# Layer-0 output products of a two-layer decoder trunk: three rounded products each, with split weights streamed through six slots

## The reference

```
h = x
for layer in range(2):
    hn = rmsnorm(h, norm_w[layer])
    h = h + (gla_rwkv_mixer if layer == 0 else swa_mixer)(hn, ...)
return rmsnorm(h, final_norm_w)

gla_rwkv_mixer:
    gq, gk, gv, g_low, rw, gate = split(hn @ w_in)
    o_a = rmsnorm_per_head(gla_chunked(gq, gk, gv, log_decay)) * gla_norm_w
    r, k, v, xw, xa = split(token_shift_mix(rw))
    o_b = layernorm_per_head(rwkv7_scan(r, decay, k, v, -kk, kk * a)) + sum(r * k * r_k) * v
    o = concat(o_a, o_b) * silu(gate)
    return o @ w_out                      # 1024 x 1024 by 1024 x 1024
```

## Time and profile before

| | |
|---|---|
| three runs | 1258.09, 1268.25, 1268.41 us, median 1268.25 |
| profiled execution | 1257.14 us |
| its span, first to last instruction | 1255.4 us |
| TensorE busy | 1164.0 us, 93% |
| VectorE, ScalarE, GpSimd busy | 40%, 30%, 31% |
| DMA | 78.91 MB, mean 63 GB/s |
| granted TensorE clock, mean | 0.969 |

### The profile page before, as it was taken

How to read it: one execution, slowest core, us unless ns; L and a number is a source line. 1 busy time by engine, 2 the same in 40 slices (tenths; PEclk the granted TensorE clock), 3 DMA queues, 4 the chain that set the end, 5 groups by cost and what they waited for, 6 DMA issues and landing times. The chain is left out here.

```text
span 1255.4 us, 32969 instructions
## 1 busy us (share of the span) xinstructions
PE 1164.0 (93%) x14856; PEld 882.5 (70%) x14856; DVE 504.4 (40%) x872; ACT 378.5 (30%) x851; POOL 384.6 (31%) x266
## 2 busy tenths in 40 slices
PE   5999999999995778999989998799999999999997
PEld 4777777888884667666666554498888885666786
DVE  5588885600002232332332322325552007887243
ACT  6343432501112223233233233311111107776111
POOL 2232323333322012122122112303333435553562
PEclk9999999999996887999999999899999999999999
DMA  6011113432404110122021011401111111111311
GB/s 241 34 35 51 34 34 106 146 99 68 134 0 188 31 52 17 50 63 56 30 59 52 6 37 40 145 30 51 49 38 46 50 34 35 35 39 36 146 51 67
DMA packets 50944, 78.91 MB, mean 63 GB/s; under 512 B 2544, under 2 KB 36096, under 8 KB 50432
## 3 DMA queue, kind: packets, MB, share of 16 engines
q1 hardware_dynamic: 50816, 76.98, 18.7%
HBM read 60.19 MB, written 16.78 MB: 61 GB/s over the span
## 5 line engine op out<-in xcount | busy, mean ns | idle before, releaser
L1469 PE MATMUL ps<-HNH,WH 128*128 128x512 f32 x736 | 289.9, 394 | 0.0
L1469 PE MATMUL ps<-HNL,WH 128*128 128x512 f32 x736 | 286.4, 389 | 0.0
L1469 PE MATMUL ps<-HNH,WL 128*128 128x512 f32 x736 | 286.4, 389 | 0.0
L1469 PEld LDWEIGHTS ps<-HNH,WH 128*128 128x128 f32 x736 | 138.2, 188 | 31.0 <-issue 2.7
L1469 PEld LDWEIGHTS ps<-HNH,WL 128*128 128x128 f32 x736 | 138.2, 188 | 30.4 <-issue 1.9
L1469 PEld LDWEIGHTS ps<-HNL,WH 128*128 128x128 f32 x736 | 138.1, 188 | 29.0
L1857 DVE CUSTOM_DVE_ANT_0 AR<-ps,GV,nsink 128x256 f32<-128x256 f32 x128 | 56.7, 481 | 97.0 <-PE ps L1667 95.9
L1050 PE MATMUL ps<-VQ,BK 128*128 128x512 f32 x128 | 66.6, 624 | 4.1 <-POOL BK L796 2.1
L1813 ACT ACTIVATE AR<-AR,nm 128x256 f32<-128x256 f32 x128 | 63.7, 500 | 18.8 <-DVE nm L1857 18.8
L1050 PE MATMUL ps<-WO,BK 128*128 128x512 f32 x128 | 64.9, 619 | 0.0
L1457 POOL CAST WH<-WA 128x1024 fp32r<-128x1024 f32 x16 | 19.1, 1191 | 138.0 <-PE ps L1469 106.9
(11 more groups left out here) (287 smaller groups left out, 2066.3 us busy)
## 6 DMA issues: line engine op xcount, KB each, us to landing
GV<-in_w1t SPq DMA_DIRECT2D x18, 512.0 KB, 3.4
AR<-in_x SPq DMA_DIRECT2D x16, 512.0 KB, 5.5
WA<-in_w0t SPq DMA_DIRECT2D x16, 512.0 KB, 3.5
RAW<-in_w0t SPq DMA_DIRECT2D x8, 512.0 KB, 3.7
bk_dram<-BK SPq DMA_DIRECT2D x1, 4096.0 KB, 17.6
RAW<-bk_dram SPq DMA_DIRECT2D x8, 512.0 KB, 5.3
h_dram<-AR SPq DMA_DIRECT2D x8, 512.0 KB, 3.3
AR<-h_dram SPq DMA_DIRECT2D x8, 512.0 KB, 7.0
```

What stands on the lines that cost most here:

```text
L1469: last = pe.matmul(out, a, b, start=(k == 0 and i == 0), stop=(k == n - 1 and i == 2))
```

## The change

The output products become three rounded products each: high by high, high x by low weights, low x by high weights. The x parts XH (ScalarE, `high_parts`) and XL (VectorE, `low_parts`) are made for each block after it is gated. The weight parts are made once, during the gate tiles: SP loads a piece of the output weights into the place of the spilled QK, VectorE splits it, SP stores both parts in device memory (`w_parts`, 8 MB), half by half. In the chunk loop six slots (WR) of 512 KB hold the two parts of one (h, k) each; SP loads the next use of a slot when its product is done (`w_used`), 128 loads in all. The place of WO in VQ is given to VS, KS, BT, AKV and RR. SP's order in a pass changes: the reloads are placed among its loads, the row block comes before the GLA values, and the value and layer-1 weights are requested at the start of pass 9.

```diff
@@ -158,14 +160,14 @@
...
+            ring = [(n, 16) for n in spilled] + [(n, 16 * KT) for n in w_stored] + [(const2_in, 16 * 2 + 8 * KT)]
...
@@ -250,6 +254,18 @@
                              spills[which].rearrange("d p a q t -> p (a q) d t"),
                              src.rearrange("p a (d t) -> p a d t", t=P)).then_inc(spilled[which], 16)

+            def load_output_weights(j):
+                if j >= 2:
+                    sp.wait_ge(w_stored[j % 2], 32 * (j // 2))
+                sp.dma_start(QK[:, j % 2, 1, :], wout[:, j, :]).then_inc(w_loaded[j % 2][0], 16)
+
+            def store_output_parts(j):
+                sp.wait_ge(w_split, 2 * j + 2)
+                for h in range(2):
+                    if h:
+                        sp.wait_ge(w_stored[j % 2], 32 * (j // 2) + 16)
+                    sp.dma_start(w_parts[h, j], QK[:, j % 2, :, h * HB:(h + 1) * HB]).then_inc(w_stored[j % 2], 16)
+
             for n in range(2, W0_TILES):
                 if n == W0_GLA + 1:

@@ -269,9 +285,19 @@
                 if n == 27:
                     sp.wait_ge(tile_kept, W0_GATE)
                     spill(2, GV[:, :, :])
+                if n == 23:
+                    sp.wait_ge(spilled[1], 16)
+                if n > 23 and n < 28:
+                    for j in range(2):
+                        store_output_parts(2 * (n - 24) + j)
+                if n >= 23 and n < 27:
+                    for j in range(2):
+                        load_output_weights(2 * (n - 23) + j)
             sp.wait_ge(spilled[0], 16)
             sp.wait_ge(gz_done, GP)
             sp.dma_start(first_keys, spills[0][0]).then_inc(bk_in0, 16)
+            for stored in w_stored:
+                sp.wait_ge(stored, 16 * KT)

         @block.gpsimd
         def _(pool):
@@ -597,10 +623,15 @@
                 e = (nrm, cum)[j % 2] if j < 2 else (e2, sw)[j % 2]
                 qk = QK[:, j // 2, j % 2, :]
                 dve.tensor_tensor(qk, qk, e, ALU.mult).then_inc(g_scaled, 1)
+            for j in range(KT):
+                there, base = w_loaded[j % 2]
+                dve.wait_ge(there, base + 16 * (j // 2 + 1))
+                split_parts(dve, QK[:, j % 2, 1, :], QK[:, j % 2, 0, :].bitcast(FR), QK[:, j % 2, 1, :].bitcast(FR),
+                            2 * j, w_split)


 def chunks0(nc, sb, sem, ctx, key_blocks, bk_in0, banks, AR, VT, VQ, GV, G, GG, small, ident, istack, bdones, maska_d, maskd_d, maskb_d,
-            SG, col, spills, spilled, w_dram, w_in, x_dram, row_in, row_turn, h1_dram, h1_out, wv1, wv_in, w1t, w1_in,
+            SG, col, spills, spilled, w_parts, ring, x_dram, row_in, row_turn, h1_dram, h1_out, wv1, wv_in, w1t, w1_in,
             W1, WV, rms, rows, H1):

     def buf(name, shape, dt=F):
@@ -634,7 +665,10 @@
     BK = key_blocks
     QK = [buf(f"QKS{i}", [P, 2, GP, P]) for i in range(2)]
     GVS = buf("GVS", [P, 2 * GP, P])
-    WO = [VQ[:, PAIRS:2 * PAIRS, :], buf("WO1", [P, PAIRS, T])[:, :, :]]
+    SLOTS = len(ring)
+    WR = buf("WR", [P, SLOTS, 2, HB], FR)
+    XH, XL = (buf(n, [P, KT, P], FR) for n in ("XH", "XL"))
+    spare = VQ[:, PAIRS:2 * PAIRS, :].rearrange("p k t -> p (k t)").rearrange("p (n c) -> p n c", c=HB)
     RB, OT = (buf(n, [P, PAIRS, P]) for n in ("RB", "OT"))
     BA, AK = ([GV[:, 2 * m + i, :].rearrange("p (a q k t) -> p a q k t", a=2, q=PAIRS, k=2) for i in range(2)]
               for m in range(2))
@@ -642,14 +676,16 @@
     X, T21 = shared(HEADS, B), shared(HEADS, B)
     XT0 = shared(HEADS, C)
     XT = [buf(f"XTL{i}", [P, HEADS, C]) for i in range(2)]
-    VS, KS, BT = ([buf(f"{n}{i}", [P, PAIRS, 2, C]) for i in range(2)] for n in ("VS", "KS", "BT"))
-    AKV, RR, U = (buf(n, [P, 2, PAIRS, C]) for n in ("AKV", "RR", "U"))
+    VS, KS, BT = ([spare[:, 2 * m + i, :].rearrange("p (q a v) -> p q a v", q=PAIRS, a=2) for i in range(2)]
+                  for m in range(3))
+    AKV, RR = (spare[:, 6 + i, :].rearrange("p (e q v) -> p e q v", e=2, q=PAIRS) for i in range(2))
+    U = buf("U", [P, 2, PAIRS, C])
     S = [buf(f"S{i}", [P, PAIRS, C]) for i in range(4)]
     SD = buf("SD", [P, PAIRS, C])
     KP, BP = shared(PAIRS, P), shared(PAIRS, P)
     OC, SQ = buf("OC", [P, HEADS, C]), buf("CSQ", [P, HEADS, C])
     OQ, GQ = SQ, SQ[:].rearrange("p h v -> p (h v)").rearrange("p (h v) -> p h v", v=P)
-    maskd = RR[:].rearrange("p e q v -> p (e q v)")[:, 0:LEVELS * C].rearrange("p (l t) -> p l t", t=C).bitcast(I32)
+    maskd = RR.rearrange("p e q v -> p (e q v)")[:, 0:LEVELS * C].rearrange("p (l t) -> p l t", t=C).bitcast(I32)
     maskb = OC[:].rearrange("p h v -> p (h v)")[:, 0:2 * C].rearrange("p (h t) -> p h t", h=2).bitcast(I32)
     OB = buf("OB", [P, PAIRS, 2, C])
     eye = OB[:, 0, 0, 0:B]
@@ -709,41 +748,57 @@
             def load_gla_values(d):
                 sp.dma_start(GVS[:], spills[2][d]).then_inc(s["gv_in"], 16)

+            def load_parts(n):
+                there, base = ring[n % SLOTS]
+                sp.dma_start(WR[:, n % SLOTS].bitcast(F), w_parts[n // KT % 2, n % KT]).then_inc(there, 16)
+
+            def replace_parts(d, h, ks):
+                for k in ks:
+                    n = product_no(d, h, k)
+                    if 0 <= d < ND and n + SLOTS < product_no(ND, 0, 0):
+                        sp.wait_ge(s["w_used"], n + 1)
+                        load_parts(n + SLOTS)
+
             for n in spilled:
                 sp.wait_ge(n, 16)
             load_gla(0)
             load_gla_values(0)
             load_keys(1)
             load_gla(1)
-            for i in range(2):
-                sp.dma_start(WO[i], w_dram[:, PAIRS * i:PAIRS * (i + 1), :]).then_inc(w_in[i], 16)
+            for n in range(SLOTS):
+                load_parts(n)
             for p in range(ND + 3):
+                if p == ND + 1:
+                    sp.wait_ge(s["o_prod"], ND)
+                    sp.dma_start(WV, wv1).then_inc(wv_in, 16)
+                    for n in range(2):
+                        sp.dma_start(W1[:, n], w1t[n]).then_inc(w1_in[n], 16)
                 if 2 <= p + 1 < ND:
                     sp.wait_ge(s["k_prod"], p)
                     sp.wait_ge(s["b_scaled"], p)
                     sp.wait_ge(s["rk"], p)
                     load_keys(p + 1)
+                replace_parts(p - 3, 1, range(5))
+                if 2 <= p + 1 < ND:
                     sp.wait_ge(s["qs_prod"], p)
                     sp.wait_ge(s["gk_scaled"], p)
                     load_gla(p + 1)
+                replace_parts(p - 3, 1, range(5, KT))
                 if 0 <= p - 3:
                     sp.wait_ge(s["out_added"], 2 * (p - 2))
                     if p - 3 >= 2:
                         sp.wait_ge(h1_out[(p - 3) % 2], 16 * ((p - 3) // 2))
                     sp.dma_start(h1_dram[:, p - 3, :].rearrange("p (k c) -> p k c", c=P), H1[:, :, tokens(p - 3)]
                                  ).then_inc(h1_out[(p - 3) % 2], 16)
-                if p + 1 < ND:
-                    sp.wait_ge(s["turned"], turn_no["gv", p])
-                    load_gla_values(p + 1)
+                replace_parts(p - 2, 0, (0,))
                 if 0 <= p - 1 < ND:
                     sp.wait_ge(s["rs_prod"], p)
                     sp.dma_start(H1[:, :, tokens(p - 1)], x_dram[:, p - 1, :].rearrange("p (k c) -> p k c", c=P)
                                  ).then_inc(row_in[p - 1], 16)
-                if p == ND + 1:
-                    sp.wait_ge(s["o_prod"], ND)
-                    sp.dma_start(WV, wv1).then_inc(wv_in, 16)
-                    for n in range(2):
-                        sp.dma_start(W1[:, n], w1t[n]).then_inc(w1_in[n], 16)
+                if p + 1 < ND:
+                    sp.wait_ge(s["turned"], turn_no["gv", p])
+                    load_gla_values(p + 1)
+                replace_parts(p - 2, 0, range(1, KT))

         @block.gpsimd
         def _(pool):
@@ -1040,17 +1095,18 @@
                 if not 0 <= d < ND:
                     return
                 for k in ks:
+                    n = product_no(d, h, k)
+                    there, base = ring[n % SLOTS]
                     if k == 0:
-                        pe.wait_ge(s["gated"], d + 1)
-                        pe.wait_ge(s["turn_kept"], turn_no["go", d])
+                        pe.wait_ge(s["x_high"], d + 1)
                         after(pe, "out_added", 2 * d + h)
-                        if d == 0 and h == 0:
-                            for loaded in w_in:
-                                pe.wait_ge(loaded, 16)
-                    last = pe.matmul(bank[5][:], SG[:, k, tokens(d)], WO[k // PAIRS][:, k % PAIRS, h * HB:(h + 1) * HB],
-                                     start=(k == 0), stop=(k == KT - 1))
-                    if k == KT - 1:
-                        last.then_inc(s["out_done"], 1)
+                    pe.wait_ge(there, base + 16 * (n // SLOTS + 1))
+                    for i, (x, w) in enumerate(((XH, 0), (XH, 1), (XL, 0))):
```

(24 more changed lines are left out.)

15 lines of the change are left out of this document (10 added, 5 removed).

## The result

The changed kernel takes 1309.9 us (median of 4 runs, 1309.7 to 1313.8) against 1268.3 for the kernel before on the same chip: ratio 1.034, 95% interval 1.030 to 1.039. The profiled execution has a span of 1312.0 us (before 1255.4) and a mean granted TensorE clock of 0.944 (before 0.969). It is slower, and lies above the forecast range. The two profiled executions differ by 56.6 us and the medians by 41.6: the profiled one of before, 1257.1 us, was faster than its four other runs (1258.1 to 1270.4), that of after the slowest of its four.

The account below looks back on a forecast made before the run. TensorE was taken as the bound, held in the loop's passes to one instruction block per 3.93 us. Loop -13.8, tail +12.9 and projection 0 gave -0.9 us: 1267 us from a median of 1268.25, range 1252 to 1284.

Parts of the forecast that it names:

- Part 3: Weight stream in the chunk loop: no wait for data in the passes, instruction blocks slowed by +0.15 us, 2 us in all.
- the one row at 397.67: Gap ending at 397.67: under 410 GB/s a block came about 4.1 us after the previous one began, +0.15.
- the third rival: Weight stream slows instruction blocks in the loop: at 4.65 us each total +15, 1283 us; at 5.37 about +40; chance 0.2.
- Part 1: Output products in the passes: one alone 0.77 us, a pair 1.44; 4.0 us less a pass, 20 us over five.
- Part 2: Passes may not outrun 3.93 us per instruction block, so 0.65 of the 20 us saving stays, 13 us.
- the average slope: Low bound for what stays of the passes' 20 us: 0.4, since 16 products lengthen a pass by 7 us.
- Part 4: Tail, the last 32 products: bound by loads of 1.30 us each, ends 12.9 us later instead of some 7 us earlier.
- Rival (b): The tail is the larger term, 1.5 us per load and a clock drop: +4 in total, 1273 us; chance 0.15.
- Part 5: Making the x parts in the passes is hidden behind other work, at 0; without that cover 1.2 us a pass.
- Part 6: Splitting weights during the gate tiles: load of tile 28 near 346, some 17 us late, within slack: 0, up to 4 us.
- rival (d): SP's rounds starve the gate tiles by 10 us, 1277 us; sign: GpSimd's casts there wait for DMA; chance 0.05.
- (a): Instructions do not limit the passes' product-rich stretch, so the whole 20 us counts: -11.1, 1257 us; chance 0.2.

## Why the prediction was wrong

**The failed step is in Part 3, "Do these loads slow the instruction blocks?"** It took +0.15 us per block from the one row at 397.67 and left the other end, 5.37 us under a DMA share of 0.57, to the third rival because waits for VectorE were mixed in. Measured in the passes: one block per 5.21 us (43 packets), and 5.6 to 6.2 in the stretches under load shown above, against 4.46 with the loads taken away. The row at 5.37 was the nearer one. The row at 397.67 was a block at the tail end of a burst, in a stretch where TensorE was busy for only about half of the window; one block there said little of a sustained stream. The stream's price in the loop was 2 us in the forecast; measured it is 40.9 us (384.7 against 343.8 without reloads). The rival was named with its mechanism and its place. Its "+40" stands behind a total of +15 that holds the tail, but worked out with the same terms 5.37 gives about +40 for the loop alone and about +52 with the tail. Measured are +39.6 and, in the profiles, +56.6. That the loop's figure is met so closely is partly luck: at the measured pace of 5.21 the same terms give only +31. The rival's middle value of 4.65 was too low.

**Two more terms were too large, unseen behind the first: the saving of Part 1 and Part 2's 0.65.** A rounded product of three inside a pass costs more than 0.77 us. Here is one at full clock, in the kernel without reloads; it takes 0.89, from its start to that of the next group.

```profile
611.02 0.73 PE L1106 MATMUL ps<-WR,XH 128*128 128x512 f32 x2
611.59 0.40 PE L1106 MATMUL ps<-WR,XL 128*128 128x512 f32 x1
611.91 0.62 PE L993 MATMUL ps<-VQ 64*64 64x64 f32 x13
```

Over its four passes a single one takes 0.87 us in the median and a pair 1.49 (forecast 0.77 and 1.44), against 1.02 and 1.82 before. The 16 products of a pass take 13.6 us against 15.8: 2.2 us less, and not 4.0. The forecast price of 0.23 holds only where such products follow each other: in that kernel's tail they start 0.69 us apart, 3 x 0.23 (769.27 to 769.96).

Of these 2.2 us hardly anything stayed. The loop without reloads is 1.3 us shorter than before, where the forecast without its 2 us for the stream was 15.8 shorter. The four passes even grew by 1.3 us each. The bound from the average slope, 0.4, lies between what the two kernels with still less product work kept (0.5 and 0.3). The added 16 pairs and the clock, which fell to 0.90 and 0.98 in two passes, may have eaten the rest; no run separates them. Part 2 gave the clock no price.

**The whole miss, by parts** (profiled executions, forecast -0.9, measured 57.3): the stream in the loop 38.9 us, the saving that did not come 14.5, the tail 2.5, the projection 2.3, together 58.2.

**Part 4 came near; its tail without loads did not.** Tail +12.9 forecast, +15.4 measured, of which the kernel without reloads shows 14.9 to be the loads (35.6 against 50.5 us). The first wait, for XH, was 2.14 us, and XL's 0.53, as in that part. The same kernel misses the forecast of a tail 7 us shorter without loads: it is as long as before (35.6 against 35.0), with waits of 5.0 us for XH, 1.0 for XL and 1.7 put down to issue, and at a clock of 0.90. Rival (b), a tail of 1.5 us per load as the cause, was the lesser term.

**Part 5 held, and Part 6 in its price.** There was no wait in the passes for XH, XL or WR. The loop began 2.3 us later, inside the 0 to 4 given. The load of tile 28 went out at 350.39, 4 us behind the forecast 346, and that was too late to be hidden. GpSimd's cast waited for it, the sign that the prediction gave for rival (d), and TensorE's tile began right after the split:

```profile
356.16 1.04 POOL L1527 CAST WH<-WA 128x1024 fp32r<-128x1024 f32 x1 [13.89 <-DMA WA<-in_w0t]
...
359.89 0.49 PE L1539 MATMUL ps<-HNH,WH 128*128 128x512 f32 x1 [1.14 <-ACT BK L414]
```

The view names ScalarE as the releaser, but GpSimd's split ended at 359.75, just before the start. It cost TensorE 1.1 us, where (d) had 10.

**The rivals.** (a), for which the Trainium skill spoke with its page Runtime: NRT & Kernel Launch, section Instruction fetch mechanics (the fetch is hidden behind the sequencer), is refuted here twice: taking the loads away from unchanged instructions takes 8.1 us off a pass, and copies that touch no tile bring the gaps back. That blocks are of 256 instructions, as the page says, holds.

## What to carry to other kernels

In a stretch of many small instructions, a DMA stream is not free because its data are in time: TensorE's instruction blocks come by DMA too, and a sustained share of 0.6 on its engines stretched blocks of 256 instructions from 4.5 to 5.2 us and cost 17% of the pass. So price a stream by the DMA time that it takes in such a stretch, keep operands resident where the instruction rate is near its limit, and reload over all 128 partitions. Of two rows that bound an unknown, take the one whose load resembles the new steady state, even if it is less clean.

Near such a floor a shorter operation gave back 0.3 to 0.5 of what it saved in two kernels here, and in the third hardly anything. Three rounded products without any reload take 1257.6 us, 0.8% under before, so with the products and the order as they are no cheaper stream would have brought this change more.

## What the runs showed that was not expected

The instruction blocks are delayed by data transfers that touch no tile and no on-chip memory (1322 us with copies from memory to memory). TensorE still asks for the copies' semaphores, but its timeline shows no wait for one in the passes. Half of the bytes cost a third of the loss over 128 partitions (18 of 52 us) and 0.65 to 0.85 of it over 64 (34 to 44 of 52). The share of DMA time went the same way, 0.40 against 0.46, though by less. And a late block costs twice: a pass lost 4.0 us in gaps and another 4.1 us in busy time, at a granted clock of 0.89 instead of 0.97.
